# Reordering weight transfers, routing and the first gather in a two-layer encoder with routed experts

## The reference

```python
grp_p = softmax(h @ w_grp + b_grp)               # 4 groups
g_w, g_idx = top_k(grp_p, 1)
sel = expert logits of group g_idx               # 8 of 32
e_w, e_idx = top_k(softmax(sel), 2)              # two experts per token
gates = one_hot(g_idx * 8 + e_idx) * (g_w * e_w / sum(e_w))
for e in range(32):
    hid = silu(h @ w_gate[e]) * (h @ w_up[e])    # 1024 -> 512
    y = y + gates[..., e:e + 1] * (hid @ w_down[e])
```

## Time and profile before

| | |
|---|---|
| time, median of 3 runs | 1213.12 us (1213.05 to 1218.9) |
| span of the profiled execution | 1210.1 us |
| time around that span, against the median | 3.0 us |
| PE busy | 993.6 us, 82% of the span |
| DVE busy | 275.5 us, 23% |
| moved by DMA | 442.92 MB, mean 366 GB/s |

### The profile page before, as it was taken

The page is one execution under the profiler, slowest core; times in us unless marked ns, Lnnn a source line. Parts: engine busy times, 40 slices in busy tenths (PEclk is TensorE's granted clock), DMA queues, the critical chain, the costliest instruction groups (busy, mean ns, idle before and its releaser), DMA issues.

```text
span 1210.1 us, 12548 instructions
## 1 busy us (share of the span) xinstructions
PE 993.6 (82%) x5208; PEld 447.0 (37%) x5208; DVE 275.5 (23%) x637; ACT 128.0 (11%) x303; POOL 3.4 (0%) x9
## 2 busy tenths in 40 slices
PE   8999999959758667976899899999597586679776
PEld 7675543413213113342385444434132132133422
DVE  1255352202102102110322452612021021021203
ACT  2024020000000000000131120200000000000001
POOL 0000000000000000000000000000000000000000
PEclk9999999989889889987999999999698898799889
DMA  9912979999999999999973327899999999999996
GB/s 375 384 71 98 388 269 426 428 419 427 429 426 430 426 428 428 425 428 423 423 300 139 122 87 327 311 426 428 427 426 428 428 430 426 431 426 429 424 423 251
DMA packets 37854, 442.92 MB, mean 366 GB/s; under 512 B 4354, under 2 KB 4738, under 8 KB 10020
## 3 DMA queue, kind: packets, MB, share of 16 engines
q1 hardware_dynamic: 37508, 442.00, 87.5%
q10 hardware_dynamic: 288, 0.13, 0.0%
HBM read 441.06 MB, written 1.05 MB: 365 GB/s over the span
## 4 chain that ended last, share of the span: by engine, by line
PE 50%; DMA 40%; DVE 3%; issue 3%; SPq 2%; ACT 0%; DVEq 0%; POOL 0%; POOLq 0%
PE psum L1608 49%; DMA sb_weights<-moe_w_down 35%; DMA sb_weights<-moe_w_gate 5%; SPq L634 1%; SPq L639 1%; PE psum L2094 0%; DVE sb_weights L1481 0%; DMA sb_cst<-ident 0%; PE psum L1637 0%; PE psum L1619 0%; PE psum L1756 0%; DVE sb_x L1501 0%; DVE sb_hT L962 0%; DVE sb_weights L1226 0%; PE psum L1992 0%
## 5 line engine op out<-in xcount | busy, mean ns | idle before, releaser
L1608 PE MATMUL psum<-sb_weights,sb_hT 128*32 128x512 f32 (+2 forms) x2336 | 464.2, 631 | 102.7 <-DMA sb_weights<-moe_w_gate 61.0
L1608 PE MATMUL psum<-sb_weights 128*32 128x512 f32 (+10 forms) x1616 | 315.8, 562 | 59.0 <-DMA sb_weights<-moe_w_down 51.1
L1608 PEld LDWEIGHTS psum<-sb_weights,sb_hT 128*32 128x32 f32 (+2 forms) x2336 | 143.1, 127 | 402.5 <-issue 323.1
L1608 PEld LDWEIGHTS psum<-sb_weights 128*32 128x32 f32 (+5 forms) x1616 | 111.5, 137 | 249.8 <-issue 202.0
L1494 DVE TENSOR_TENSOR sb_x<-sb_x,psum 128x512 f32<-128x512 f32 x84 | 57.7, 687 | 277.2 <-PE psum L1608 277.2
L1608 PE MATMUL psum<-sb_hT,sb_weights 128*128 128x256 f32 (+1 forms) x400 | 88.8, 380 | 2.1 <-DVE sb_hT L962 2.1
L1608 PE MATMUL psum<-sb_weights,sb_hn 128*128 128x192 f32 (+2 forms) x448 | 71.3, 320 | 13.8 <-issue 12.5
L1608 PEld LDWEIGHTS psum<-sb_hT,sb_weights 128*128 128x128 f32 (+1 forms) x400 | 74.0, 187 | 14.9 <-DVE sb_hT L962 2.7
L1608 PEld LDWEIGHTS psum<-sb_weights,sb_hn 128*128 128x128 f32 x448 | 69.1, 203 | 15.6 <-issue 15.6
L1486 DVE COPY sb_weights<-psum 96x512 f32<-96x512 f32 (+1 forms) x20 | 13.7, 686 | 194.4 <-PE psum L1608 194.4
L1481 DVE TENSOR_TENSOR sb_weights<-sb_weights,psum 96x512 f32<-96x512 f32 (+1 forms) x22 | 15.1, 684 | 164.5 <-PE psum L1608 164.5
(11 more groups left out here) (191 smaller groups left out, 335.2 us busy)
## 6 DMA issues: line engine op xcount, KB each, us to landing
sb_weights<-moe_w_gate SPq DMA_DIRECT2D x60, 2048.0 KB, 25.2
sb_weights<-moe_w_down SPq DMA_DIRECT2D x58, 2048.0 KB, 27.0
sb_weights<-moe_w_up SPq DMA_DIRECT2D x52, 2048.0 KB, 27.2
sb_weights<-moe_w_up SPq DMA_DIRECT2D x24, 1024.0 KB, 17.4
sb_weights<-od_w_in_units SPq DMA_DIRECT2D x6, 2048.0 KB, 28.0
sb_weights<-ev_w_in_units SPq DMA_DIRECT2D x5, 2048.0 KB, 25.2
sb_weights<-moe_w_gate SPq DMA_DIRECT2D x16, 512.0 KB, 6.8
sb_weights<-moe_w_down SPq DMA_DIRECT2D x6, 1024.0 KB, 24.6
```

Source lines behind the costliest of these rows:

```text
L1608: return nc.tensor.matmul(o, l, r, start=start, stop=stop, skip_group_check=True)
```

## The change

The edits, in both layers:

1. The first round's gate matrices take units 0 to 2 as the input projection frees them, the output projection's two units go to units 3 and 4, up 2 to unit 5. Behind the five arena units SP issues the first half of up 0 into scratch (`up_rows`, the place of three buffers that are first written later). After the output projection come the second half of up 0, up 1, and the first half of the fourth expert's up matrix.
2. The last group of the output projection is made of two halves of 256 columns (`q` 0 and 1), each with its own bank, add, transposes, copy and (second half) a square sum of its own. The semaphores of the two layers are merged.
3. Routing: `first_max` goes; the group is picked as before, then other groups' logits are pushed far down, and `max` and `max_index` (eight largest of 32, and their places) give the two experts.
4. The first gather is cut in four pairs of blocks; two stand ahead of the gate products, two between them. The 0/1 matrix of round 0 is made in two parts.
5. `keep_warm` runs 3 products and not 5.

```diff
+PAIR_GATHER_BANKS = (7, 5, 6, 4)
...
+OUT_UNITS = (3, 4)
...
+QUARTER_OUT_BANKS = (7, 5)
+QUARTER_TURN_BANKS = (1, 4)
...
-        for h in range(2):
-            sp.wait_ge(proj_psum[layer], 2 * h + 2)
-            sp.dma_start(unit[h], w_outs[layer][h]).then_inc(out_full, 16)
+        for c in range(LIGHT):
+            sp.wait_ge(proj_psum, 2 * IN_UNITS * layer + 2 * c + 2)
+            known(layer, "gate", c, unit[SLOT["gate"] + c], main.full["gate"])
+        for h, c in enumerate(OUT_UNITS):
+            sp.wait_ge(proj_psum, 2 * IN_UNITS * layer + 2 * c + 2)
+            sp.dma_start(unit[c], w_outs[layer][h]).then_inc(out_full, 16)
...
-        sp.wait_ge(proj_psum[layer], 6)
-        known(layer, "gate", 2, unit[SLOT["gate"] + 2], main.full["gate"])
-        for k in range(LIGHT):
-            sp.wait_ge(proj_psum[layer], 8 + 2 * k)
-            known(layer, "up", k, unit[SLOT["up"] + k], main.full["up"])
+        sp.wait_ge(proj_psum, 2 * IN_UNITS * layer + 12)
+        known(layer, "up", 2, unit[SLOT["up"] + 2], main.full["up"])
         sp.wait_ge(*arena_free[layer])
         for k in range(LIGHT):
             known(layer, "down", k, unit[SLOT["down"] + k], main.full["down"])
         known(layer, "gate", LIGHT, held, held_full)
         known(layer, "down", LIGHT, held_down, held_down_full)
-        sp.wait_ge(out_psum[layer], 4)
-        for k in range(2):
-            known(layer, "gate", k, unit[SLOT["gate"] + k], main.full["gate"])
+        half_rows(layer, "up", 0, 0, up_rows, up_rows_full)
+        sp.wait_ge(out_psum, 5 * layer + 5)
+        half_rows(layer, "up", 0, 1, unit[SLOT["up"]][:, UNIT // 2:UNIT], main.full["up"])
+        known(layer, "up", 1, unit[SLOT["up"] + 1], main.full["up"])
+        half_rows(layer, "up", LIGHT, 0, unit[SLOT["up"]][:, 0:UNIT // 2], up_half_full)
...
         add_half(0, 0)
         turned_half(0, 1)
         inverse(n, 0)
         scale_x(n, 0)
+        add_quarter(0)
         turned_half(1, 0)
-        add_half(1, 1)
-        turned_half(1, 1)
+        turned_quarter(0)
+        add_quarter(1)
+        turned_quarter(1)
         inverse(n, 1)
...
+        others, groups = rt_oh, logit[:, :, 0:4]
+        a = rt_a[:, :, 0:4]
+        chained(V.tensor_reduce(gmax, groups, AX_X, ALU.max))
+        chained(V.tensor_tensor(a, groups, gmax.to_broadcast([P, 2, 4]), ALU.is_ge))
+        chained(V.scalar_tensor_tensor(out=a, in0=a, scalar=-64.0, in1=iota4, op0=ALU.mult, op1=ALU.add))
+        chained(V.tensor_reduce(first, a, AX_X, ALU.min))
+        chained(V.tensor_tensor(others, a, first.to_broadcast([P, 2, 4]), ALU.not_equal))
+        chained(V.scalar_tensor_tensor(out=rt_b.rearrange("p t (g e) -> p t g e", g=4),
+                                       in0=others.unsqueeze(3).to_broadcast([P, 2, 4, 8]), scalar=MASKED,
+                                       in1=logit[:, :, 4:36].rearrange("p t (g e) -> p t g e", g=4),
                                        op0=ALU.mult, op1=ALU.add))
-        first_max(rt_o2, rt_sel, 8, m2, iota8)
-        V.tensor_tensor(ex[:, :, 4:5], m2, m1, ALU.subtract).then_inc(pre_exp, 1)
-        chained(V.tensor_tensor(rt_a[:, :, 0:8], rt_o1, rt_o2, ALU.add))
-        oh4 = rt_oh.unsqueeze(3).to_broadcast([P, 2, 4, 8])
-        M4 = rt_M.rearrange("p t (g e) -> p t g e", g=4)
-        G4 = rt_G.rearrange("p t (g e) -> p t g e", g=4)
-        V.tensor_tensor(M4, oh4, rt_a[:, :, 0:8].unsqueeze(2).to_broadcast([P, 2, 4, 8]), ALU.mult
-                        ).then_inc(mask_done, 1)
+        unchained(V.max(rt_top[:, 0], rt_b[:, 0]))
+        chained(V.max(rt_top[:, 1], rt_b[:, 1]))
+        unchained(V.max_index(places[:, 0], rt_top[:, 0], rt_b[:, 0]))
+        chained(V.max_index(places[:, 1], rt_top[:, 1], rt_b[:, 1]))
+        chained(V.tensor_tensor(rt_pair, iota32, places[:, :, 0:2].unsqueeze(3).to_broadcast([P, TILES, 2, 32]),
+                                ALU.is_equal))
+        G = rt_G
+        V.tensor_tensor(rt_M, rt_pair[:, :, 0], rt_pair[:, :, 1], ALU.add).then_inc(mask_done, 1)
+        unchained(V.tensor_tensor(ex[:, :, 0:4], groups, gmax.to_broadcast([P, 2, 4]), ALU.subtract))
+        V.tensor_tensor(ex[:, :, 4:5], rt_top[:, :, 1:2], rt_top[:, :, 0:1], ALU.subtract).then_inc(pre_exp, 1)
...
+        first_one_hot(main, rt_R)
+        gathered_pairs(layer, main, layer * MOE_GROUPS, layer)
...
+        chained(V.tensor_tensor(rt_pair, rt_pair, rt_s[:, :, 4:6].unsqueeze(3).to_broadcast([P, TILES, 2, 32]),
+                                ALU.mult))
+        chained(V.tensor_tensor(G, rt_pair[:, :, 0], rt_pair[:, :, 1], ALU.add))
...
+            if q == 0:
+                turn_x(layer, 0, 0)
+                turn_x(layer, 0, 1)
+            for at, b in enumerate((4, 5, 6, 7, 0, 1, 2, 3)):
+                if q and at == 0:
                     turn_x(layer, 1, 0)
                     pe.wait_ge(wr_scaled, 2)
                     logits(layer, 0, 0)
                     logits(layer, 0, 1)
-                if i == 0 and at in turned:
-                    pe.wait_ge(*turned[at])
-                ins = mm(psum[:, 4 + i], mixT[:, b, t * P:(t + 1) * P],
-                         w[b // 4][:, b % 4, half * HALF:(half + 1) * HALF], at == 0, at == 7)
-            ins.then_inc(done_sem, 1)
+                if q and at == 4:
+                    turn_quarter(layer, 0)
+                ins = mm(psum[:, QUARTER_OUT_BANKS[q], 0:QUARTER], mixT[:, b, P:2 * P],
+                         w[b // 4][:, b % 4, (2 + q) * QUARTER:(3 + q) * QUARTER], at == 0, at == 7)
+            ins.then_inc(out_psum, 1)
...
-        turn_x(layer, 1, 1)
+            pe.wait_ge(cst_loaded, 2 * 16)
         logits(layer, 1, 0)
+        turn_quarter(layer, 1)
         logits(layer, 1, 1)
-        keep_warm(5)
+        keep_warm(3)
...
+    def gather_pair(s, gn, after, b, k):
+        if b == 0:
+            pe.wait_ge(s.early_sel, k + 1)
+        bank = PAIR_GATHER_BANKS[b]
+        if bank in SCATTER_BANKS:
+            pe.wait_ge(s.x_added, after * 4 + (3 + SCATTER_BANKS.index(bank)))
+        for j in (2 * b, 2 * b + 1):
+            for t in range(TILES):
+                ins = mm(psum[:, bank, (j % 2) * ROUND_SLOTS:(j % 2 + 1) * ROUND_SLOTS],
+                         hn[:, t, j * P:(j + 1) * P], sel[:, t, 0:ROUND_SLOTS], t == 0, t == TILES - 1)
+        ins.then_inc(s.gath_psum if b % 2 else s.early_gath, 1)
...
+            first_rows = up_rows.rearrange("p (j n) -> p j n", j=KT // 2)
+            if kind == "up" and frees:
+                pe.wait_ge(up_rows_full, 16 * (k + 1))
             for j in range(KT):
                 if by_rows and j % 4 == 0:
                     pe.wait_ge(last_up[j // 4], 16 * LIGHT * (k + 1))
+                if kind == "gate" and first and j in (2, 4):
+                    gather_pair(s, gn, k * ROUNDS, j // 2 + 1, k)
                 if kind == "gate" and first and j % 4 == 0:
+                    pe.wait_ge(s.early_hsel, k * 2 + (j // 4 + 1))
+                elif kind == "gate" and first and j % 4 == 2:
                     pe.wait_ge(s.hsel_done, gn * 4 + (j // 4 + 1))
...
+                    w = first_rows if kind == "up" and frees and e == 0 and j < KT // 2 else ws[e]
+                    ins = mm(psum[slots * e:slots * (e + 1), bank], hsel[:, j, at:at + slots], w[:, j, :],
...
-        gather_round(s, k * MOE_GROUPS, k * ROUNDS, 0)
+        for b in range(2):
+            gather_pair(s, k * MOE_GROUPS, k * ROUNDS, b, k)
```

215 lines of the change are left out of this document (126 added, 89 removed).

## The result

The changed kernel takes 1209.68 us (median of 6 runs, 1207.24 to 1213.06) where the forecast said 1205.8, in a range of 1202 to 1210. The kernel before, run beside it, had a median of 1217.42 (6 runs, 1213.05 to 1220.24). The ratio is 0.9948, with a 95% interval from 0.993 to 0.9966: 0.5% faster, by 6.3 us (4.1 to 8.5). Against the median that the forecast started from, 1213.12, it is only 3.4 us. The time lies in the range, the change against that base is not the 7.3 us forecast. Both numbers will be explained.

The account below looks back on a forecast made before the run. The prediction took the DMA transfer queue to pace the routed part. Gains of 3.35 us in layer 0 and 3.95 in layer 1, together 7.3, were to bring 1213.1 to 1205.8 us, range 1202 to 1210.

Parts of the forecast that it names:

- the sum: Landing of round 1's downs: 2.1 + 1.25 = 3.35 us in layer 0, 2.7 + 1.25 = 3.95 in layer 1, together 7.3.
- X: How much earlier the first round's down products end in each layer: 1.25 us.
- the queue's term: Older transfers queued ahead of round 1's downs, to be taken off: 2.1 us in layer 0, 2.7 in layer 1.
- The time around the span: Time outside the profiled span, taken to stay at 3.0 us.
- the same steps: Layer 0 was to go through layer 1's steps from output projection to downs, 603.45 us earlier, with the same gain.
- rival D: PE's clock falls in the routing: 1234 us if it stays down, one dip costs 2.9 (1211.6); chance 0.04.
- it never empties before the layer's end: From the issue of round 2's gates on, the transfer queue was to stay filled until the layer ends.
- Mask: Routing, first reduce to mask: 2.73 us where it took 4.56, gained 1.8.
- Two maxima and two searches: Two MAX and two MAX_INDEX in the routing, 0.22 us each with hand-off, 0.88 for four.
- rival A: MAX and MAX_INDEX in the routing cost above 0.4 us each: 1207.1 to 1209.6 us; chance 0.20.
- Gather: First gather of round 0 starts 2.1 us earlier, at 765.1 in layer 1; DVE's last pair copied at 772.8.
- The chain: DVE's gate values and `put_in_order` ahead of the hidden product: 10.95 us where it took 11.26, ending at 783.75.

Follow-up runs that it names:

- the late tail: Changed kernel with the last five operations of `put_in_order` moved behind the weighting of the first group; 1210.18 us.
- the old order: Changed kernel with the old order of weights (output weights in units 0 and 1, gates 0 and 1 fetched behind the output projection); 1225.59 us.
- e2: Changed kernel with five keep-warm products in place of three; 1211.64 us.
- e3: Changed kernel with four keep-warm products in place of three; 1210.3 us.
- e6: Changed kernel with four keep-warm products and the last five operations of `put_in_order` moved behind the weighting of the first group; 1205.61 us.
- e12: The kernel of e6 once more, unchanged, beside the same kernel with a whole first gather; 1207.67 us.
- e14: The kernel of e6 once more, beside the changed kernel on the same chip; 1208.41 us against 1210.59.
- e8: Changed kernel with the first gather whole again instead of in pairs, the rest kept; 1210.71 us.
- the two small edits: Four keep-warm products in place of three, and the last five operations of `put_in_order` moved later, both in the changed kernel; 1205.61, 1207.67 and 1208.41 us.
- e10: Changed kernel with the old routing chain (two maxima found by reductions) and five keep-warm products; 1217.8 us.

## Why the prediction was wrong

The time of 1209.68 us lies in the range, but not because the sum was right, and it misses 1205.8 by 3.9 us. By the medians that is mostly the base: 1216.7 over all 84 runs of the kernel before, 3.6 above 1213.12. By the spans of the two shown profiles, 1202.8 forecast and 1208.0 measured, 5.2 us are missing: 2.0 at the start, 1.5 from X in layer 0, 0.7 and 1.0 from the queue's term in the two layers.

**The base.** The forecast took 7.3 us off a profile of span 1210.1 and off 1213.12 us. The kernel before was timed 84 times in all beside the others, on different chips, with medians of 1215.1 to 1217.4; 12 of the 84 took 1213.12 or less, and its second profile has 1216.2. The shown profile had the quick start, no fall in layer 0's routing and none in mixer 1. The time around the span was 1.8 us and not 3.0, which takes 1.2 off the miss in the time, by luck.

**X in layer 0** is the step that failed. The forecast said that layer 0 has the same steps, with X = 1.25. The downs were issued 72.47 us behind the arena transfer, and 72.20 before: X = -0.27. The clock fell in the gather, and PE lost 1.6 us. The step says nothing of the clock, which the prediction had only as rival D, at 0.04 and for idle times like 7.60 us. D's mechanism was right and its point of onset wrong: 0.79 us and 0.42 us with 1.08 us of small products between were enough, in layer 0 of all five profiles with that pair of holes (three of the changed kernel, one of the late tail, one of the old order). With the hole of 0.79 filled the clock stayed up there (e2, e3, e6, e12, e14). D's price, 2.9 us for a dip, was too high for this one. The Trainium skill (TensorE: Matmul & The Clock Gate, Part 1) has the low clock as the default that activity lifts. The trace agrees as far as it goes: after idle times of this size the clock does not always stay up.

Like for like, this loss is on both sides. Against the second profile of before, which fell as well, X is 73.83 - 72.47 = 1.36, and layer 0 is 3.0 us shorter (504.2 to 501.2), nearly the 3.35 of the sum.

**The queue's term** was mis-sized in both layers. It was to be 2.1 and 2.7 us, the landing of the downs behind their issue less 8.0 us. What the layers gained beyond X is 1.36 us in layer 0 (1.1 + 0.27), or 1.6 like for like, and 1.7 in layer 1 (3.0 - 1.27). A part is that the downs landed 8.35 and 8.36 us after their issue and not 8.0. The rest is that this one transfer came forward by more than the layer did: 1.47 us in layer 0 where the layer gained 1.1, and 3.57 in layer 1, where the transfer three places later came 2.9 forward (a gate landed at 820.50, 5.54 us behind the one before it, where 4.9 is usual) and those a round later 3.1. The queue did not run empty in that stretch, so the sentence that it never empties before the layer's end is not what failed. The window of it, in the columns of the earlier trace rows:

```profile
800.00:836.00 36.00, 35.12 (x221) 13.96 (x218) 6.82 (x11) 1.67 (x3) 0.00 (x0) 1.00 1.00 426
```

So the landing of a single transfer was too generous a measure for what the queue holds; why it runs ahead is not shown.

**Layer 1**, but for that, went as written, step by step. Mask 2.4 us earlier relative to the arena (1.96 of it in the routing itself, 1.8 forecast). Two maxima and two searches 0.78 us from start to start (0.88 forecast; rival A falls). Gather 2.6 us earlier (2.1), but 7.86 us from its start to DVE's last copy (7.25 forecast: two pairs took 2.00 for 1.86, one pair 1.13 for 0.93, two blocks of gates 1.92 for 1.75); that the two cancel is luck. The chain 10.96 (10.95). Hidden product directly behind it. X = 65.61 - 64.34 = 1.27 (1.25). That DVE's chain became the limit is the price of the pieces (e8).

The rule that a search for places is two operations (the Trainium skill, Vector Engine (DVE) Microarchitecture Reference, 3.9) holds in the trace: a load of 0.07 to 0.09 and a search of 0.18 us. The 0.44 us that the forecast worked out from it did not come: the load is shorter than the reduce, and the second load started 0.10 us after the first search, ahead of its end.

**Start to end.** 6.0 us like for like (3.0 in each layer) against 7.3 forecast, and 6.3 (4.1 to 8.5) by the ratio of the runs. The queue argument was right in kind (the gain is what the queue held ahead of the downs, plus X). The order alone gave 1.6 us in layer 0 with X at nothing, and each later cut in X was found again in layer 0: the two small edits brought the issue from 72.5 to 70.2 and the layer from 501.2 to between 498.5 and 499.1. In layer 1, 0.7 of issue was worth 0.5.

What stays open: why the fall comes every time in layer 0 and in two of five in layer 1, where the same two holes stand; and why the start takes about 2 us more in nine of the seventeen profiles, where the record of the full clock begins later. The halved last output group and the shorter routing were not run alone.

## What to carry to other kernels

A single profile is one draw: before subtracting from it, see whether the baseline's own times agree with each other, and look for places where its PE was lucky. When an edit shortens work that covers a wait of PE, look at the idle that it leaves, and fill every such hole of the stretch together, because a fall of the clock that is taken from one hole can come in the next one. And where the transfer queue has run dry ahead of an issue, the issue decides, and the order of earlier transfers has paid all that it can.

## What was not expected of the hardware

- Behind idle times of PE under 2 us the granted clock fell to 0.50 (1.2 GHz), mostly for some 3 us: behind 0.80 + 0.42 us (five of five profiles in layer 0, two of five in layer 1), behind 0.65 + 0.62 (layer 0, two of three), behind 0.80 or 0.95 + 0.62 (both layers of e8), behind 1.04 + 0.42 (layer 1 of e10, not layer 0), behind 1.60 (four of twelve layers), behind 1.90 (one of two), behind 0.78 at the end of layer 1's output projection (two of four). One fall costs 1.6 us in the gather. Behind a single 0.90 none was seen.
- The first 16 products behind the start's idle of 0.78 us took 3.72 us in eight profiles and 5.4 to 6.1 in nine. The record of the clock begins, at 2.4 GHz, between 7.6 and 9.0 us in the eight and between 12.7 and 14.2 us in the nine. Ahead of its first entry the windows print 1.00 whatever the clock was, so there the durations tell it and the clock column doesn't.
- MAX8 over 128x32 took 0.18 to 0.20 us, and a second, independent one started 0.11 us after the first.
